# A tuned decoder kernel: the first conditioning's shift summed by TensorE, half of its tokens scaled by ScalarE

## The chip, the cores and the metric

One Trainium2 chip, one of its cores. The metric is the device time of one execution in microseconds, as a median over runs. All data is f32; some matmul operands are split into a high and a low fp32r part.

## The reference, cut to what matters

Two decoder layers over 256 tokens of width 1024. Each begins with an adaptive conditioning; of layer 0 only the first lines concern the change:

```
c_act = silu(c)                                   # (1, 1024)
mod   = c_act @ w_mod[l] + b_mod[l]               # (1, 6*1024): sh1, sc1, g1, sh2, sc2, g2
h     = x * (1.0 + sc1) + sh1                     # 256 tokens, 1024 wide
y     = hybrid_mixer(h, w_in[l], ...)             # h @ w_in, then attention and gated linear attention
x     = layer_norm(ALPHA * x + (1.0 + g1) * y, ...)
```

After the mixer come a SwiGLU of width 2816 (layer 0) and a mixture of experts (layer 1), about the last 770 us of the kernel.

## The kernel before, in words

All engines run programs of their own, and semaphores tie them together. The order of the work is written out by hand.

**First conditioning.** The 1024 rows of w_mod are cut into 8 blocks k of 128 rows (128 partitions), and of each block only the 1024 columns of the shift (a = 0) and of the scale (a = 1) are loaded first: 16 pieces of 512 KB, in the order of FIRST_ROWS (line 90), with the two halves of x behind pieces 10 and 12 (line 91, loop at line 375). SyncE issues them, and behind them the weights of the projections (`unit_load`, line 412). Before the change VectorE takes each piece as it lands (line 1463 on): it multiplies it by c_act's column k and adds it to `ycat[:, a, :]`, so that each partition holds a partial sum. TensorE then sums over partitions (`sum_chunk`, line 983): for each 128 columns, four products of 32 columns of the accumulator with a column of ones (`mm4`, line 938). Once both are summed, VectorE writes the conditioning into the table modT (line 1453). Between its two sums TensorE transposes x (`transposed_tokens`, 16 transposes into banks 0 to 3) and the table of norms (line 992).

**First tokens.** `modulate_first` (line 1497) makes hfull = x^T * scale + shift, a block kt of 128 columns of the model at a time, on VectorE alone. `project` for unit U_BQ (line 1017 on) multiplies hfull by the raw weights in f32: for ct = 0 and 1, the eight kt in order, each waiting for its block of hfull.

**What follows.** The units of the projection have a ring of four buffers. Unit u (from 4 on) is loaded once unit u - 4 is projected (line 414), so that unit 4 (U_IQ1) waits for unit 0 (U_BQ). ScalarE rounds a unit to its high part (`conv_unit`), VectorE subtracts (`low_unit`), and TensorE projects with three fp32r products (`mm3`). The tokens get a high and a low part too (`high_of_tokens`, `low_of_tokens`). SyncE's queue also carries the conditioning rows of later stages (`load_mod_rows`); rows 0 and 1 wait for the first sums (mod_ps), the others mostly for a buffer to be read (row_rd, VectorE's `condition_rows`). GpSimd (POOL) loads the gate's bias and the norm rows; it starts that once the first conditioning's partial sums are ready.

**Names and lines.** Piece loads L376 and L381, units L424, rows L409. Partial sums L1466 and L1469, sums over partitions L942, token transposes L951, table modT L1456, modulation L1501, U_BQ L1022, unit splits L651 (ScalarE) and L1552 (VectorE), token parts L692 and L1525, later rows L1539 and L1541, ScalarE's decay bias L711.

Of the kernel before, what the change touches and what calls it, by code (L numbers as in the profile page):

```python
# [21 lines left out]
ACT = mybir.ActivationFunctionType  # L22
AX = mybir.AxisListType

P = 128
D = 1024
KT = D // P
T = 256
# [61 lines left out]
FIRST_ROWS = [(1, k) for k in range(4)] + [(a, k + 4 * a) for k in range(4) for a in (1, 0)] + [(0, k) for k in range(4, 8)]  # L90
# [18 lines left out]
def hybrid_decoder(nc, x, c, w_in, w_a2, b_a, gla_norm_g, w_out, w_mod, b_mod, ln_g, ln_b,  # L109
# [3 lines left out]
    with ctx:  # L113
# [418 lines left out]
        def _(pool):  # L532
# [71 lines left out]
            pool.wait_ge(s["mod_sum"], 2)  # L604
# [23 lines left out]
        def _(act):  # L628
# [57 lines left out]
            def high_of_tokens(ph):  # L686
                for h in ((1, 0) if ph else (0, 1)):
                    if ph and h:
                        act.wait_ge(s["hfull_a"], ph * KT)
                    else:  # L690
                        act.wait_ge(s["hfull"], ph * KT + (KT if ph else 4 * h + 4))
                    A(hT_H[:, 4 * h:4 * h + 4, :], hfull[:, 4 * h:4 * h + 4, :], ACT.Copy).then_inc(s["hT_H"], 1)  # L692
# [110 lines left out]

            mixer(0)
# [130 lines left out]
        def _(pe):  # L935
# [29 lines left out]
            def token_tile(ph, t, kt):  # L965

                if kt < 4:
                    pe.wait_ge(s["hfull"], ph * KT + 4 * t + kt + 1)
                else:
                    pe.wait_ge(s["hfull_a"], (ph - 1) * KT + 4 * t + kt - 3)  # L970
# [17 lines left out]
            pe.wait_ge(s["mod_sum"], 1)  # L988
            sum_chunk(ycat[:, 1, :], bank[6][:, KT:2 * KT])
# [5 lines left out]
            pe.wait_ge(s["mod_sum"], 2)  # L995
            sum_chunk(ycat[:, 0, :], bank[6][:, 0:KT]).then_inc(s["mod_ps"], 1)

            def project(l, u, between=None):
                b = bank[4 + u % 2]
                if u < PLAIN:  # L1000
# [16 lines left out]
                    else:  # L1017
                        for ct in range(2):
                            for kt in range(KT):
                                if ct == 0:  # L1020
                                    pe.wait_ge(s["hfull"], kt + 1)
# [421 lines left out]
        def _(dve):  # L1443
# [17 lines left out]
            before = [0, 0]  # L1461
            for i, (a, k) in enumerate(FIRST_ROWS):
                dve.wait_ge(mod_ld[i], 16)
# [3 lines left out]
                else:  # L1467
                    dve.wait_ge(s["dve_chain"], before[a])
                    last = V.scalar_tensor_tensor(out=acc, in0=w, scalar=c_act[:, k:k + 1], in1=acc,  # L1469
                                                  op0=ALU.mult, op1=ALU.add)  # L1470
                if k == KT - 1:
                    last.then_inc(s["mod_sum"], 1)
                else:
                    last.then_inc(s["dve_chain"], 1)
                    n[0] += 1
                    before[a] = n[0]
                if i == 8:
# [19 lines left out]
            def modulate_first():  # L1497

                for kt in range(KT):
# [21 lines left out]
            def low_of_tokens(ph):  # L1521
                for i, h in enumerate((1, 0) if ph else (0, 1)):
# [503 lines left out]
```

## Time and profile before

| | |
|---|---|
| median of 3 runs | 1275.26 us (1275.22 to 1275.42) |
| the profiled execution's own time | 1272.66 us |
| its span | 1270.9 us |
| mean granted TensorE clock | 0.983 |
| TensorE matmul busy | 1183.0 us (93%) |
| VectorE busy | 569.0 us (45%) |
| ScalarE busy | 302.1 us (24%) |
| DMA, mean | 318 GB/s |

The profile is one execution. Its times are from the first to the last instruction (the span). PE is TensorE's matmuls, PEld its weight loads, DVE VectorE, ACT ScalarE, POOL GpSimd, SP SyncE; a "q" behind a name is that engine's queue issuing a transfer. A busy share is an average over stages. This change touches the first 50 us, so timelines and the chain of waits over that stretch say more than the page's totals. The granted clock is TensorE's, as a share of 2.4 GHz.

### The profile page before, as it was taken

To read this page: it belongs to the slowest core of one execution; us is meant where nothing else is said; L and a number is where in the kernel's file an instruction comes from. 1 tells how busy PE (TensorE), PEld (TensorE's weight loads), DVE (VectorE), ACT (ScalarE), POOL (GpSimd) and SP (SyncE) were. 2 spreads that over 40 slices of the span, in tenths; PEclk is the share of its full clock that TensorE was granted. 3 is DMA by queue.
4 is the path that set the end of the run, shared out by engine and by line. 5 is a ranking of instruction groups with operands and counts; after the bars stand their busy time and mean duration, and the time that the engine had idled before them with its cause. 6 is when DMAs were issued, how large, how long until landed. Compare 5 with 4: busy or idle time off the path is not lost.

```text
span 1270.9 us, 26228 instructions
## 1 busy us (share of the span) xinstructions
PE 1183.0 (93%) x11180; PEld 641.1 (50%) x11180; DVE 569.0 (45%) x913; ACT 302.1 (24%) x521; POOL 43.8 (3%) x84
## 2 busy tenths in 40 slices
PE   1889889999999898799999999999999999999996
PEld 1879867788878787523334323334233233333332
DVE  6799988677758999421021020111210210210224
ACT  0557243433336571310010010100100100100100
POOL 2101010000011010000000000000000000000001
PEclk9899989999999999799999999999999999999998
DMA  9973868899727648889999989999989999999950
GB/s 340 312 257 116 290 227 312 322 347 329 244 68 239 201 167 315 334 326 371 413 364 414 394 299 414 412 364 411 388 310 411 410 364 404 396 362 411 379 233 34
DMA packets 149083, 403.60 MB, mean 318 GB/s; under 512 B 19964, under 2 KB 71328, under 8 KB 137696
## 3 DMA queue, kind: packets, MB, share of 16 engines
q1 hardware_dynamic: 146720, 395.16, 82.5%
q0 software_dynamic: 2240, 6.68, 1.4%
q8 instruction: 92, 1.51, 0.5%
q14 instruction: 31, 0.25, 0.1%
HBM read 400.75 MB, written 1.05 MB: 316 GB/s over the span
## 4 chain that ended last, share of the span: by engine, by line
PE 75%; DVE 13%; DMA 6%; issue 3%; ACT 2%; SPq 1%; POOL 0%; DVEq 0%; ACTq 0%
PE bank L1349 36%; PE bank L1368 18%; PE bank L337 5%; PE bank L339 4%; PE bank L338 4%; DVE mod_acc L1541 3%; DMA raw_u<-in_ffn_w_up_dram 2%; DMA u_raw<-in_w_in_dram 2%; DVE u_low L1552 2%; PE bank L1331 1%; DMA mod_first<-in_w_mod_dram 1%; PE bank L1228 1%; DVE score L1596 1%; PE bank L1339 1%; PE bank L1022 1%
## 5 line engine op out<-in xcount | busy, mean ns | idle before, releaser
L1349 PE MATMUL bank<-raw_w,xg 128*32 128x512 f32 (+1 forms) x4608 | 462.9, 557 | 4.5 <-issue 2.5
L1349 PEld LDWEIGHTS bank<-raw_w,xg 128*32 128x32 f32 x4608 | 147.1, 110 | 304.7 <-issue 304.6
L1368 PE MATMUL bank<-raw_w,heT 128*32 128x512 f32 x2112 | 232.9, 593 | 0.0
L1915 DVE TENSOR_TENSOR he<-he,bank 128x256 f32<-128x256 f32 (+1 forms) x72 | 25.6, 384 | 369.4 <-ACT he L869 369.4
L869 ACT ACTIVATE he<-bank 128x256 f32<-128x256 f32 (+1 forms) x72 | 21.2, 367 | 542.8 <-PE bank L1349 542.8
L1368 PEld LDWEIGHTS bank<-raw_w,heT 128*32 128x32 f32 x2112 | 67.3, 110 | 150.5 <-issue 149.3
L1942 DVE SCALAR_TENSOR_TENSOR ycat<-bank,gate_tab,ycat 128x512 f32<-128x512 f32 x36 | 25.4, 747 | 173.0 <-PE bank L1340 171.1
L1541 DVE SCALAR_TENSOR_TENSOR mod_acc<-mod_row,c_act,mod_acc 128x1024 f32<-128x1024 f32 x70 | 89.8, 1283 | 6.8 <-DVE mod_acc L1541 0.9
L337 PE MATMUL bank<-u_high,hT_H 128*128 128x256 f32 x256 | 75.4, 294 | 4.9 <-DVE u_low L1552 3.5
L339 PE MATMUL bank<-u_high,hT_L 128*128 128x256 f32 x256 | 72.8, 284 | 0.0
L338 PE MATMUL bank<-u_low,hT_H 128*128 128x256 f32 x256 | 72.6, 284 | 0.0
L337 PE MATMUL bank<-gu_H,hT_H 128*128 128x512 f32 x160 | 64.8, 405 | 0.0
L651 ACT ACTIVATE u_high<-u_raw 128x2048 fp32r<-128x2048 f32 x26 | 49.7, 1912 | 59.6 <-DMA u_raw<-in_w_in_dram 45.6
L339 PE MATMUL bank<-gu_H,hT_L 128*128 128x512 f32 x160 | 63.1, 395 | 0.0
L338 PE MATMUL bank<-gu_L,hT_H 128*128 128x512 f32 x160 | 63.1, 394 | 0.0
L1552 DVE TENSOR_TENSOR u_low<-u_raw,u_high 128x2048 fp32r<-128x2048 f32 x26 | 59.2, 2286 | 3.0 <-ACT u_high L651 2.8
L337 PEld LDWEIGHTS bank<-u_high,hT_H 128*128 128x128 f32 x256 | 49.0, 191 | 8.0 <-DVE u_low L1552 4.6
L337 PE MATMUL bank<-hT_H,u_high 128*128 128x256 f32 x176 | 50.6, 287 | 2.1 <-DVE u_low L1550 2.1
L1926 DVE TENSOR_TENSOR y_sum<-y_sum,bank 32x512 f32<-32x512 f32 x48 | 32.9, 685 | 42.7 <-ACT y_sum L883 42.1
L339 PE MATMUL bank<-hT_H,u_low 128*128 128x256 f32 x176 | 49.6, 282 | 0.0
L338 PE MATMUL bank<-hT_L,u_high 128*128 128x256 f32 x176 | 49.5, 281 | 0.0
L338 PEld LDWEIGHTS bank<-u_low,hT_H 128*128 128x128 f32 x256 | 49.0, 192 | 0.7 <-issue 0.7
(284 smaller groups left out, 1378.7 us busy)
## 6 DMA issues: line engine op xcount, KB each, us to landing
raw_w<-in_moe_w_down_dram SPq DMA_DIRECT2D x88, 1024.0 KB, 8.6
raw_w<-in_moe_w_gate_dram SPq DMA_DIRECT2D x128, 512.0 KB, 8.5
raw_w<-in_moe_w_up_dram SPq DMA_DIRECT2D x128, 512.0 KB, 9.8
mod_row<-in_w_mod_dram SPq DMA_DIRECT2D x80, 512.0 KB, 6.4
raw_w<-in_moe_w_gate_dram SPq DMA_DIRECT2D x64, 384.0 KB, 5.6
raw_w<-in_moe_w_up_dram SPq DMA_DIRECT2D x64, 384.0 KB, 6.8
u_raw<-in_w_in_dram SPq DMA_DIRECT2D x20, 1024.0 KB, 7.5
raw_d<-in_ffn_w_down_dram SPq DMA_DIRECT2D x11, 1024.0 KB, 10.1
```

The costliest lines, as they stand in the source:

```text
L337: nc.tensor.matmul(out_ap, aH, bH, start=first, stop=False)
L338: nc.tensor.matmul(out_ap, aH, bL, start=False, stop=False)
L339: return nc.tensor.matmul(out_ap, aL, bH, start=False, stop=last)
L651: A(dst[:], src[:], ACT.Copy).then_inc(s["wH"], 1)
L869: A(he[:, g, 0:w].rearrange("s (j b c) -> s j b c", b=2, c=32), bank[g][:, 0:w].rearrange("s (j c b) -> s j b c", b=2, c=32), ACT.Silu).th ...
L1349: last = mm(bank[g][32 * q:32 * q + 32, 0:2 * HALF[c]].rearrange("s (m j r) -> s m j r", m=2, r=64), xg[:, i, k, 32 * g:32 * g + 32], cols ...
L1368: last = mm(bank[3 + g][32 * q:32 * q + 32, :], heT[(par + c) % 2][:, g, 2 * a + b, :], W[:, b, h * 512:(h + 1) * 512], start=(c == 0 and ...
L1541: last = V.scalar_tensor_tensor(out=acc, in0=row[:], scalar=c_act[:, k:k + 1], in1=acc, op0=ALU.mult, op1=ALU.add)
L1552: V.tensor_tensor(L[:], src[:], H[:].bitcast(F32), ALU.subtract).then_inc(s["wL"], 1)
L1915: V.tensor_tensor(h, h, bank[g][:, w:2 * w].rearrange("s (j c b) -> s j b c", b=2, c=32), ALU.mult).then_inc(s["m_hid"], 1)
L1926: last = V.tensor_tensor(a, a, bank[3 + g][64 * h + 32:64 * h + 64, :], ALU.add)
L1942: V.scalar_tensor_tensor(out=a, in0=bank[b][:], scalar=gate_tab[:, t, bass.ds(E, 1)], in1=a, op0=ALU.mult, op1=ALU.add).then_inc(s["m_acc" ...
```

## The change

FIRST_ROWS now goes through k, with the scale's piece ahead of the shift's. VectorE sums only the scale's pieces. TensorE forms the shift itself: for each landed piece k, eight products of 128 columns of raw weights with the column c_act[:, k], accumulated over k in bank 6 (`shift_row`). Six of the eight pieces stand ahead of the transposes, two behind them, and the scale's sum over partitions is last. modT follows it. Blocks 4 to 7 of the tokens are modulated by ScalarE, ahead of its first unit split, and signalled by hfull_a; U_BQ takes the blocks in the order 0, 4, 1, 5, 2, 6, 3, 7. The tokens' high and low parts go through the halves in the order 1, 0 in every phase. GpSimd waits for mod_ps in place of mod_sum.

```diff
--- before.py
+++ after.py
@@ -87,7 +87,7 @@
 ROWS_AT_STEP = (0, 5, 5, 5, 5, 4, 4, 4, 4, 4, 0)
 MOD_AT_STEP = {3: 5, 5: 6, 6: 7, 8: 8}
 
-FIRST_ROWS = [(1, k) for k in range(4)] + [(a, k + 4 * a) for k in range(4) for a in (1, 0)] + [(0, k) for k in range(4, 8)]
+FIRST_ROWS = [(a, k) for k in range(KT) for a in (1, 0)]
 X_AFTER = (9, 11)
 
 HF0, HF1, YC0, YC1, X0 = range(5)
@@ -601,7 +601,7 @@
                     link(pool.tensor_scalar(rms[:, t, :], ssq[:, t, :], 1.0 / B_DV, EPS, ALU.mult, ALU.add))
                     pool.tensor_tensor(rms[:, t, :], rms[:, t, :], half_neg[:, 4:8], ALU.pow).then_inc(s["rms"], 1)
 
-            pool.wait_ge(s["mod_sum"], 2)
+            pool.wait_ge(s["mod_ps"], 1)
             gate_bias(0, 2, g_row)
             mixer(0)
             norm_power(0)
@@ -684,11 +684,8 @@
                 last.then_inc(s["evac"], 1)
 
             def high_of_tokens(ph):
-                for h in ((1, 0) if ph else (0, 1)):
-                    if ph and h:
-                        act.wait_ge(s["hfull_a"], ph * KT)
-                    else:
-                        act.wait_ge(s["hfull"], ph * KT + (KT if ph else 4 * h + 4))
+                for h in (1, 0):
+                    act.wait_ge(s["hfull_a" if h else "hfull"], ph * KT + 4)
                     A(hT_H[:, 4 * h:4 * h + 4, :], hfull[:, 4 * h:4 * h + 4, :], ACT.Copy).then_inc(s["hT_H"], 1)
 
             def normalise(ph):
@@ -801,6 +798,11 @@
                         conv_unit(l, NIN + 2)
                 conv_unit(l, NIN + 3)
 
+            act.wait_ge(s["modT"], 1)
+            for kt in range(4, KT):
+                act.wait_ge(s["xT_ps"], kt // 2 + 1)
+                A(hfull[:, kt, :], bank[kt // 2][:, (kt % 2) * T:(kt % 2 + 1) * T], ACT.Identity,
+                  scale=modT[:, 8 + kt:9 + kt], bias=modT[:, kt:kt + 1]).then_inc(s["hfull_a"], 1)
             mixer(0)
 
 
@@ -965,9 +967,9 @@
             def token_tile(ph, t, kt):
 
                 if kt < 4:
-                    pe.wait_ge(s["hfull"], ph * KT + 4 * t + kt + 1)
+                    pe.wait_ge(s["hfull"], ph * KT - 4 + 4 * t + kt + 1)
                 else:
-                    pe.wait_ge(s["hfull_a"], (ph - 1) * KT + 4 * t + kt - 3)
+                    pe.wait_ge(s["hfull_a"], ph * KT - 4 + 4 * t + kt - 3)
 
             def gate_sum(m, banks):
 
@@ -985,15 +987,26 @@
                 for k in range(KT):
                     last = mm4(o[:, k:k + 1], acc[:, k * P:(k + 1) * P], ones[:, 0:1], start=True, stop=True)
                 return last
-            pe.wait_ge(s["mod_sum"], 1)
-            sum_chunk(ycat[:, 1, :], bank[6][:, KT:2 * KT])
+
+            def shift_row(k):
+
+                pe.wait_ge(mod_ld[FIRST_ROWS.index((0, k))], 16)
+                for j in range(KT):
+                    mm(bank[6][:, j:j + 1], mod_first[:, k, j * P:(j + 1) * P], c_act[:, k:k + 1],
+                       start=(k == 0 and j == 0), stop=(k == KT - 1 and j == KT - 1))
+
+            pe.wait_ge(s["cact"], 1)
+            for k in range(6):
+                shift_row(k)
             pe.wait_ge(s["cols_rd"], 1)
             pe.wait_ge(s["stage2_ld"], 32)
             nc.tensor.transpose(bank[7][:, 0:P], stage2[:], ident[:]).then_inc(s["stageT"], 1)
             pe.wait_ge(s["x_ld"], 32)
             transposed_tokens(x_sb, "xT_ps")
-            pe.wait_ge(s["mod_sum"], 2)
-            sum_chunk(ycat[:, 0, :], bank[6][:, 0:KT]).then_inc(s["mod_ps"], 1)
+            shift_row(6)
+            shift_row(7)
+            pe.wait_ge(s["mod_sum"], 1)
+            sum_chunk(ycat[:, 1, :], bank[6][:, KT:2 * KT]).then_inc(s["mod_ps"], 1)
 
             def project(l, u, between=None):
                 b = bank[4 + u % 2]
@@ -1016,9 +1029,9 @@
                             last = mm(b[q:q + BLK, 0:T], u_raw[u % 4][:, kt, 0:BLK], hfull[:, kt, :], start=(kt < 4), stop=(kt >= 4))
                     else:
                         for ct in range(2):
-                            for kt in range(KT):
+                            for kt in (0, 4, 1, 5, 2, 6, 3, 7):
                                 if ct == 0:
-                                    pe.wait_ge(s["hfull"], kt + 1)
+                                    pe.wait_ge(s["hfull" if kt < 4 else "hfull_a"], kt % 4 + 1)
                                 last = mm(b[:, ct * T:(ct + 1) * T], u_raw[u % 4][:, kt, ct * P:(ct + 1) * P], hfull[:, kt, :],
                                           start=(kt == 0), stop=(kt == KT - 1))
                     last.then_inc(s["proj"], 1)
@@ -1458,23 +1471,21 @@
 
 
             dve.wait_ge(s["cact"], 1)
-            before = [0, 0]
             for i, (a, k) in enumerate(FIRST_ROWS):
+                if a == 0:
+                    continue
                 dve.wait_ge(mod_ld[i], 16)
                 w, acc = mod_first[:, k, a * D:(a + 1) * D], ycat[:, a, :]
                 if k == 0:
                     last = V.tensor_scalar(acc, w, c_act[:, 0:1], None, ALU.mult)
                 else:
-                    dve.wait_ge(s["dve_chain"], before[a])
                     last = V.scalar_tensor_tensor(out=acc, in0=w, scalar=c_act[:, k:k + 1], in1=acc,
                                                   op0=ALU.mult, op1=ALU.add)
                 if k == KT - 1:
                     last.then_inc(s["mod_sum"], 1)
                 else:
-                    last.then_inc(s["dve_chain"], 1)
-                    n[0] += 1
-                    before[a] = n[0]
-                if i == 8:
+                    link(last)
+                if k == 4:
                     dve.wait_ge(s["stageT"], 1)
                     V.tensor_copy(cols[:], bank[7][:, 0:P]).then_inc(s["cols_rd"], 1)
             dve.wait_ge(s["cols_rd"], 1)
@@ -1496,7 +1507,7 @@
 
             def modulate_first():
 
-                for kt in range(KT):
+                for kt in range(4):
                     dve.wait_ge(s["xT_ps"], kt // 2 + 1)
                     V.tensor_scalar(hfull[:, kt, :], bank[kt // 2][:, (kt % 2) * T:(kt % 2 + 1) * T],
                                     modT[:, 8 + kt:9 + kt], modT[:, kt:kt + 1], ALU.mult, ALU.add).then_inc(s["hfull"], 1)
@@ -1519,7 +1530,7 @@
                 dve.wait_ge(s["lnm"], ph + 1)
 
             def low_of_tokens(ph):
-                for i, h in enumerate((1, 0) if ph else (0, 1)):
+                for i, h in enumerate((1, 0)):
                     k = slice(4 * h, 4 * h + 4)
                     dve.wait_ge(s["hT_H"], 2 * ph + i + 1)
                     V.tensor_tensor(hT_L[:, k, :], hfull[:, k, :], hT_H[:, k, :].bitcast(F32), ALU.subtract)\
```

## Rows read from the trace of the kernel before

**Rows 1.** The chain of waits, 20 to 62 us (start us, us, what).
```profile
9.30 16.00 DMA mod_first<-in_w_mod_dram
...
30.84 0.75 PE bank L942 x59
...
31.69 0.25 DVE modT L1456 x2
...
32.66 10.09 PE bank L1022 x32
...
42.76 6.01 DMA u_raw<-in_w_in_dram
...
48.80 1.93 ACT u_high L651
```

**Rows 2.** Timeline of VectorE, 21 to 56 us (start us, us, instructions, idle before).
```profile
21.54 2.56 DVE L1469 SCALAR_TENSOR_TENSOR ycat<-mod_first,c_act,ycat 128x1024 f32<-128x1024 f32 x2 [1.10 <-DMA mod_first<-in_w_mod_dram]
25.33 5.45 DVE L1469 SCALAR_TENSOR_TENSOR ycat<-mod_first,c_act,ycat 128x1024 f32<-128x1024 f32 x4 [1.24 <-DMA mod_first<-in_w_mod_dram]
...
31.97 3.71 DVE L1501 TENSOR_SCALAR hfull<-bank,modT 128x256 f32<-128x256 f32 x8
...
45.66 2.29 DVE L1552 TENSOR_TENSOR u_low<-u_raw,u_high 128x2048 fp32r<-128x2048 f32 x1 [2.09 <-ACT u_high L651]
...
50.74 2.29 DVE L1552 TENSOR_TENSOR u_low<-u_raw,u_high 128x2048 fp32r<-128x2048 f32 x1 [0.73 <-ACT u_high L651]
52.95 2.67 DVE L1541 SCALAR_TENSOR_TENSOR mod_acc<-mod_row,c_act,mod_acc 128x1024 f32<-128x1024 f32 x2
```

**Rows 3.** Timeline of TensorE's matmuls, 0 to 32 us.
```profile
8.54 0.47 PE L981 MATMUL bank<-ident,stage 128*128 128x128 f32 x1 [8.54 <-POOL half_neg L563]
...
22.87 1.03 PE L942 MATMUL bank<-ones,ycat 128*32 128x1 f32 x64 [13.86 <-DVE ycat L1469]
...
24.11 3.64 PE L951 MATMUL bank<-ident,x_sb 128*128 128x128 f32 x16
...
30.84 0.71 PE L942 MATMUL bank<-ones,ycat 128*32 128x1 f32 x64 [3.09 <-DVE ycat L1469]
```

**Rows 4.** Timeline of weight loads in narrow stretches: strips, then first and first two full-width.
```profile
22.87 0.95 PEld L942 LDWEIGHTS bank<-ones,ycat 128*32 128x32 f32 x64 [14.15 <-DVE ycat L1469]
...
32.63 0.29 PEld L1022 LDWEIGHTS bank<-hfull,u_raw 128*128 128x128 f32 x1 [1.16 <-DMA u_raw<-in_w_in_dram]
...
32.63 0.50 PEld L1022 LDWEIGHTS bank<-hfull,u_raw 128*128 128x128 f32 x2 [1.16 <-DMA u_raw<-in_w_in_dram]
...
46.37 0.19 PEld L1102 LDWEIGHTS bank<-baT,wa 128*128 128x128 f32 x1 [3.12 <-ACT baT L677]
...
46.37 0.30 PEld L1102 LDWEIGHTS bank<-baT,wa 128*128 128x128 f32 x2 [3.12 <-ACT baT L677]
```

**Rows 5.** Windows: stretch, us, PE PEld DVE ACT POOL busy (records), PEclk, DMA share, GB/s.
```profile
24.10:27.80 3.70, 3.65 (x17) 3.25 (x16) 2.36 (x2) 0.00 (x0) 0.00 (x0) 1.00 1.02 409
32.60:38.50 5.90, 5.84 (x14) 4.71 (x15) 3.08 (x7) 2.52 (x2) 4.55 (x9) 0.50 1.08 365
38.60:42.75 4.15, 4.15 (x23) 3.38 (x26) 3.88 (x3) 1.19 (x2) 0.00 (x0) 1.00 1.04 420
46.30:47.10 0.80, 0.73 (x3) 0.68 (x4) 0.80 (x1) 0.02 (x1) 0.00 (x0) 1.00 1.06 372
...
509.60:513.00 3.40, 2.96 (x73) 2.64 (x74) 1.11 (x5) 1.80 (x5) 0.00 (x0) 0.50 1.02 406
513.00:516.40 3.40, 3.40 (x75) 3.05 (x76) 1.54 (x10) 0.94 (x2) 0.00 (x0) 0.50 1.03 410
```

**Rows 6.** Timeline of ScalarE, 35 to 52 us.
```profile
37.80 1.99 ACT L692 ACTIVATE hT_H<-hfull 128x1024 fp32r<-128x1024 f32 x2
43.65 1.91 ACT L651 ACTIVATE u_high<-u_raw 128x2048 fp32r<-128x2048 f32 x1 [3.86 <-DMA u_raw<-in_w_in_dram]
...
50.62 0.82 ACT L711 ACTIVATE dec<-bank,cols 128x256 f32<-128x256 f32 x2
```

## The prediction

> **What bounds the kernel now.** I read the chain of waits first, from 9 to 56 us, then each engine's timeline over that stretch. The chain [rows 1] shows no free piece at the start. The first conditioning's weights arrive until VectorE can take its last four blocks at 25.33; then come TensorE's sums over partitions (30.84), the table modT (31.69) and the first projection U_BQ, 10.09 us long. The chain leaves U_BQ for a transfer: SyncE may issue the block of unit 4 (U_IQ1) only when U_BQ is through (42.76), the block lands 6.01 us later, ScalarE splits it, VectorE subtracts. What counts for the rest of the kernel is when VectorE gets at U_IQ1's low part, at 50.74 [rows 2]. Behind that point VectorE has no long gap, and the shift of this point is the shift of the end.
>
> VectorE's timeline [rows 2] also gives the arrivals. It restarts on landings at 21.54 (block 11) and 25.33 (block 13); blocks 12 and 13 and half of x, 512 KB each, lie between, so one piece takes 3.8/3 = 1.27 us, and block 16 lands near 25.3 + 3 x 1.27 = 29.1. VectorE's last operation began at 29.5. So **only some 1.7 us** of VectorE work (30.8 - 29.1) can be taken off behind the last landing.
>
> **What one single-column product costs.** Each f32 matmul is two weight loads and two matmul records (64 records for 32 products in each of the two sums [rows 3]). The old sums load 32 columns at a time, into four strips: 64 loads in 0.95 us. The new products load all 128 columns for one column of output, so the load is the price. No such product is in the trace; its load is. At a granted clock of 0.50 (1.2 GHz), the first full-width f32 load takes 0.29 us, two take 0.50; at 1.00 (2.4 GHz), 0.19 and 0.30 [rows 4, 5]. One more load costs 0.21 us or 0.11 us. The one-column matmul hides under the next load: the strips' 64 loads, four abreast, are 16 steps of 0.055 us for a quarter of the columns, in line with 0.21 for all. So a row block (8 products, 16 loads) costs 16 x 0.213 = 3.4 us at half clock or 1.76 us at full, and the shift's blocks come every 2.54 us (every second piece). Bounds for a load: 0.055 us below (if full width cost no more than a strip), 0.21 above.
>
> **The clock at that time.** The windows print 1.00 over 24.1 to 27.8 [rows 5], but 16 transposes take 3.64 us there, 0.21 us apart, and the sum of 22.87 takes 1.03 us where the same sum at 30.84 takes 0.71 [rows 3]. I read half clock up to the transposes and full clock after them. It is at 0.50 again over 32.6 to 38.5 and at 1.00 behind that [rows 5]. So the products begin cold. Do they raise the clock? In 509.6 to 513.0 TensorE was busy 2.96 of 3.40 us, most of the 73 records being the router's products of eight columns, and the clock was still 0.50 in the next stretch [rows 5], where the dense transposes had raised it near 28. [...] I take it that they don't raise it.
>
> **The change, step by step** (against the profiled execution).
> 1. TensorE is free for products from 8.54 + 0.47 = 9.0 [rows 3]; the first shift block lands by about 29.1 - 16 x 1.27 = 8.8. Six blocks at 3.4 us are 20.5 us: **29.5**, where the sixth landed at 22.8. TensorE is the bound now, not the transfers.
> 2. One stage transpose and the 16 token transposes, 17 x 0.213 = 3.6: 33.1, against 27.75 before.
> 3. The transposes raise the clock, as before. Blocks 7 and 8, long landed: 32 loads at 0.11 = 3.5 us: 36.6. They may start a little cold or end so.
> 4. The scale's sum, now last: 0.71 to 1.03, then 0.14 + 0.24 to modT [rows 1, 3]: **about 37.8**, against 31.93. That is +5.9 us.
> 5. VectorE loses 8 operations of at most 1.36 us each (5.45 / 4), some 10 us. Worth nothing: its last block is piece 15 now, landed at 27.8, done at 29.1, and it then waits for TensorE.
> 6. Modulation: 8 VectorE operations took 3.71 us [rows 2]; four now run on ScalarE, 0.41 us each by the nearest row, 128x256 out of PSUM with a bias [rows 6]. TensorE takes a block's first half in 0.85 us at half clock and 0.43 at full, VectorE gives one per 0.46: the split, with its new order of blocks, is worth at most 0.3 us.
> 7. U_BQ follows modT by 0.7 us as now: 38.5. Its 32 records move 256 columns each, twice a transpose's, so 0.427 us at half clock and 0.213 at full; 14 at the one and 18 at the other make 9.8, near the 10.09 measured, and 14 is what the window at 0.50 counts [rows 1, 5]. All at half is 13.7, all at full 6.8. It starts cold again after the narrow products; I take 9.3 (between 8.6 and 9.8). End **47.8** against 42.75, +5.0.
> 8. SyncE issues unit 4 at 47.8. The two mod_row blocks ahead of it, tied to the same modT sums, are through by then, where they were not before: 5.3 us in place of 6.01. Lands at 53.1, VectorE reaches U_IQ1 at 55.1 against 50.74: **+4.3 us**.
> 9. What stands in between is covered. ScalarE's split of U_BK sits behind its new modulation and runs at 39.5, not 36; then two token halves in 1.99 us, and the split of U_IQ0 at 43.5, when it ran at 43.65 anyway [rows 6]. VectorE's lows and two conditioning rows end near 51.4, before 55.1. TensorE's U_BK starts some 3.4 us late, less than VectorE. POOL now waits for the sums: its bias row, pads and row loads shift by 6 us and are needed much later. Swapping the halves of the tokens' high and low parts moves no end, since U_BK needs both.
>
> Sum: 1272.66 + 4.3 = 1277.0 for the profiled execution. The runs' median stands 2.6 us above it; on that scale 1275.26 + 4.3 = **1279.6 us**.
>
> **A rule beside the rows.** The rows give 0.21 us for a full-width f32 load at half clock and 0.11 at full. The Trainium skill, "TensorE: Matmul & The Clock Gate", LDWEIGHTS, has columns/1.2 ns, 107 ns for 128 columns, whatever the clock. By that rule TensorE would keep up; the row at half clock is twice that, and decides. The same page says of transposes (Part 4) that they don't count as busy for the clock; the sums before and after the transposes speak against it here, and by that rule step 3 would run cold, which is the second rival.
>
> **Rivals.**
> (a) *Clock stays low through blocks 7 and 8* (the transposes fall so that they don't raise it, or they count for less). 32 loads at 0.213 are 6.8, 3.3 more than above: modT at 41.1, and the end +7.6 us: 1282.9. For: the transposes stand between narrow work now. Against: the rise near 28.
> (b) *TensorE keeps up* (not slower). It decides at 2.54 us per block, 0.159 us a load: if a load of these takes 0.11 us at either clock, or the products raise the clock themselves, a block takes 1.76 us. Block 6 ends by 24.6, transposes by 28.2, blocks 7 and 8 at 31.6, modT at 32 to 33. U_BQ then ends between 40 and 43.1. A late end costs 0.3 us; an early one gives next to nothing, as VectorE, behind the U_IQ0 block that lands at 43.65, is not free before 50.74 - 0.73 = 50.0, and its next two rows wait on loads issued behind the last two. 1275.1 to 1275.6. For: loads cost 0.11 at full clock. Against: half clock at the start. (The skill's LDWEIGHTS rule above would give this case.)
> (c) *Faster.* The same, and U_IQ0's block also lands sooner because POOL's row loads no longer meet it. VectorE's gaps of 2.09 and 0.73 us [rows 2] are all there is: at best -2.8, 1272.5.
> (d) *Absorbed*: the delay arises, but a later wait on a transfer takes up part: +1 to +2.5.
>
> **Numbers.** The forecast 0.50 (1278.5 to 1281), (a) 0.24, (b) 0.17, (c) 0.03, (d) 0.06. A measurement of this kernel can tell about 0.2%, 2.5 us, from no change. Faster 0.03; same is (b) and (d) and a little of the forecast's low edge, 0.24; slower 0.73. The range 1275.1 to 1283.5 takes in (a) and most of (b).
>
> **What would show it.** Right: TensorE's product records back to back from 9 to about 29.5, weight loads of 128 columns 0.21 us apart; transposes ending near 33; modT near 38; U_BQ's end and unit 4's issue near 48. Wrong: gaps between the blocks of products (TensorE keeps up), loads nearer 0.11 or 0.055 us apart, or modT before 33. If modT is late and the end isn't, (d) holds.

## The result, and the profile after

The median of six runs is 1280.98 us, against 1275.24 us for six runs of the kernel before beside them: ratio 1.0053, 95% interval [1.0039, 1.0066]. The change costs 5.7 us by the medians, 6.8 by the ratio: half a per cent. The forecast was +4.3.

| | before | after |
|---|---|---|
| profiled execution's own time | 1272.66 us | 1287.19 us |
| its span | 1270.9 us | 1285.5 us |
| mean granted TensorE clock | 0.983 | 0.982 |
| TensorE matmul busy | 1183.0 us | 1212.3 us |
| VectorE busy | 569.0 us | 557.5 us |

The profiled execution of after is the slowest of its six, and that of before (1272.66) lies below all six runs beside after (1274.76 to 1276.59), so the 14.6 us between the spans is not the change's price. VectorE's instructions of the two traces, lined up with each other, say where it arises: after is 7.6 us late at 60 us, 9.5 at 540, 11.2 at 560, 12.6 behind the first of the experts' two loop jumps and 14.6 behind the second.

TensorE's matmuls in the timeline of after, to 52 us:

```profile
8.68 3.41 PE L995 MATMUL bank<-c_act,mod_first 128*128 128x1 f32 x16
12.81 17.23 PE L995 MATMUL bank<-c_act,mod_first 128*128 128x1 f32 x80 [0.72 <-DMA mod_first<-in_w_mod_dram]
...
30.14 3.62 PE L953 MATMUL bank<-ident,x_sb 128*128 128x128 f32 x16
33.56 6.83 PE L995 MATMUL bank<-c_act,mod_first 128*128 128x1 f32 x32
40.31 1.03 PE L944 MATMUL bank<-ones,ycat 128*32 128x1 f32 x64
42.45 8.68 PE L1035 MATMUL bank<-hfull,u_raw 128*128 128x256 f32 x32 [1.11 <-DVE hfull L1512]
```

Six blocks of products run from 8.68 to 29.9 with one gap of 0.72 us for a landing: 96 records, 0.215 us each. Blocks 7 and 8 run at the same 0.213 us a record; the transposes ahead of them didn't bring the full clock. The level is read off this spacing, which is that of the loads at a recorded 0.50 in [rows 4, 5]: the windows of a profile print 1.00 until its first recorded change of the clock, and that of after is a rise at 45.6 us. The sum (1.03) answers to the cold one of [rows 3] (cold: at half clock), and modT's first write comes at 41.49 (VectorE's timeline, next), 9.8 us later than in [rows 1].

VectorE's timeline of after over the same stretch:

```profile
29.58 1.28 DVE L1482 SCALAR_TENSOR_TENSOR ycat<-mod_first,c_act,ycat 128x1024 f32<-128x1024 f32 x1 [1.27 <-DMA mod_first<-in_w_mod_dram]
...
41.49 0.24 DVE L1469 SCALAR_TENSOR_TENSOR modT<-bank,cols 128x8 f32<-128x8 f32 x2 [10.62 <-PE bank L944]
41.76 1.90 DVE L1512 TENSOR_SCALAR hfull<-bank,modT 128x256 f32<-128x256 f32 x4
...
58.32 2.29 DVE L1563 TENSOR_TENSOR u_low<-u_raw,u_high 128x2048 fp32r<-128x2048 f32 x1 [2.77 <-ACT u_high L651]
```

The 10.62 us in front of modT are the VectorE time that the change freed: it became idle time. U_IQ1's low part begins at 58.32, not 50.74 [rows 2]: +7.6. ScalarE's timeline shows its new work and then the block it waits for:

```profile
41.76 1.93 ACT L804 ACTIVATE hfull<-bank,modT 128x256 f32<-128x256 f32 x4 [35.81 <-DVE modT L1469]
...
56.38 1.91 ACT L651 ACTIVATE u_high<-u_raw 128x2048 fp32r<-128x2048 f32 x1 [3.79 <-DMA u_raw<-in_w_in_dram]
```

SyncE issued that block at 51.17, when U_BQ was through; it landed 5.2 us later.

This is the course of rival (a), to 0.6 us: modT written by 41.7 (41.1 there), +7.6 at U_IQ1. A second execution of the same kernel, `r_after` below, took the course of the main forecast. Both are this kernel.

### The profile page after: what moved, and what is told of

It is laid out like the page before. It is cut to its first block, busy times and chain, and to the rows that moved or that the text cites. A ratio compares the mean times of both kernels' runs of the same rounds, so it can differ in the third digit from the quotient of the medians.

```text
span 1285.5 us, 26343 instructions
## 1 busy us (share of the span) xinstructions
PE 1212.3 (94%) x11244; PEld 669.1 (52%) x11244; DVE 557.5 (43%) x901; ACT 303.8 (24%) x525; POOL 43.8 (3%) x84
## 4 chain that ended last, share of the span: by engine, by line
PE 69%; DVE 6%; DMA 2%; issue 1%; ACT 1%; POOL 0%; SPq 0%; DVEq 0%; ACTq 0%
PE bank L1362 36%; PE bank L1381 18%; PE bank L337 3%; PE bank L339 3%; PE bank L338 3%; PE bank L1344 2%; DVE u_low L1563 1%; DMA u_raw<-in_w_in_dram 1%; PE bank L1352 1%; DMA raw_u<-in_ffn_w_up_dram 1%; DVE mod_acc L1552 1%; PE bank L1353 1%; DVE score L1607 0%; PE bank L944 0%; PE bank L977 0%
## 5 line engine op out<-in xcount | busy, mean ns | idle before, releaser
L651 ACT ACTIVATE u_high<-u_raw 128x2048 fp32r<-128x2048 f32 x26 | 49.7, 1913 | 28.2 <-PE bank L339 14.8
```

The costliest lines, as they stand in the source:

```text
L651: A(dst[:], src[:], ACT.Copy).then_inc(s["wH"], 1)
```

## The experiments

All ratios are to the kernel before on the same chip. Where a mark is named (U_IQ1's low part at 50.74 before, or modT's first write at 31.69), it is from one profiled execution.

**`r_after`: the change again**, for a second profile.

> The changed kernel unaltered, for a second profiled execution on the same chip. The first profile has VectorE 7.5 us late at U_IQ1's low part and another 7 us that arise after 540 us, while its timed runs are 5.7 us slower. If the late 7 us belong to one execution, this one's shift stays at 7 to 8 us or less to the end; if they follow from the change, it grows again in the experts. Timed 1280.5 to 1281.5.

Measured (four runs): 1282.94 us, ratio 1.0062 [1.0045, 1.0078]; the medians lie 8.4 us apart, and the time is above the range that I expected. Timelines of TensorE and VectorE, and a window behind blocks 7 and 8 (granted clock: third number from the end):

```profile
33.38 3.89 PE L995 MATMUL bank<-c_act,mod_first 128*128 128x1 f32 x32
39.27 9.56 PE L1035 MATMUL bank<-hfull,u_raw 128*128 128x256 f32 x32 [1.10 <-DVE hfull L1512]
...
38.31 0.24 DVE L1469 SCALAR_TENSOR_TENSOR modT<-bank,cols 128x8 f32<-128x8 f32 x2 [7.68 <-PE bank L944]
56.00 2.29 DVE L1563 TENSOR_TENSOR u_low<-u_raw,u_high 128x2048 fp32r<-128x2048 f32 x1 [3.63 <-ACT u_high L651]
...
37.20:43.90 6.70, 5.60 (x76) 4.65 (x76) 2.75 (x7) 5.32 (x7) 5.12 (x10) 0.51 0.95 335
```

The clock came up behind the transposes this time: the same 32 records in 3.89 us, 0.12 each, and it is recorded as back at half from 37.3 on. modT's first write is at 38.31, U_IQ1 +5.3. So the clock at blocks 7 and 8 came out differently in two executions of one kernel, and was worth 3 us at modT and 2.3 at U_IQ1. The other profiles say how often: behind the 16 transposes the clock came up in four of the twelve that entered them cold (before, `r_after`, `e_act_only`, `e_strips_old`) and stayed at half in eight; `e_wide` was up before. Before's second sum at 0.71 us [rows 3] is the rarer course: in `b_pad`, `b_hold2`, `e_hold` and `e_hold2` the same sum takes 1.03.

The growth behind 540 us, too, came back in this profile (1.7 us before 560, then 1.5 and 1.4 at the experts' jumps).

**`e_strips`: the same products in four strips of 32 columns**, so that a load costs what the old sums' loads did.

```diff
-                    mm(bank[6][:, j:j + 1], mod_first[:, k, j * P:(j + 1) * P], c_act[:, k:k + 1],
+                    mm4(bank[6][:, j:j + 1], mod_first[:, k, j * P:(j + 1) * P], c_act[:, k:k + 1],
...
```

> The changed kernel with one edit: each of the shift's products is cut into four strips of 32 output columns (64 weight loads of 32 columns per row block in place of 16 of 128). Theory A (the full-width f32 weight load at half clock, 0.213 us, sets the delay): a row block costs 1.0 us in place of 3.4, below the 2.54 us between its arrivals, so TensorE waits for each block; the last ends 1 us behind its landing near 29, modT at 31 to 32, and the time is that of the kernel before, 1275.2 within 1 us. Theory B (the delay comes from the new order, transposes and the scale's sum behind six blocks, or from POOL's and the mod_row loads tied to modT, or from ScalarE's modulation): it stays at 1279 to 1281.

Measured: 1279.22 us, ratio 1.0034 [1.0021, 1.0047]. TensorE's and VectorE's timelines:

```profile
20.26 1.03 PE L944 MATMUL bank<-c_act,mod_first 128*32 128x1 f32 x64 [0.89 <-DMA mod_first<-in_w_mod_dram]
...
31.61 1.03 PE L944 MATMUL bank<-c_act,mod_first 128*32 128x1 f32 x64 [0.59 <-DMA mod_first<-in_w_mod_dram]
...
33.64 0.24 DVE L1469 SCALAR_TENSOR_TENSOR modT<-bank,cols 128x8 f32<-128x8 f32 x2 [2.08 <-PE bank L944]
52.68 2.29 DVE L1563 TENSOR_TENSOR u_low<-u_raw,u_high 128x2048 fp32r<-128x2048 f32 x1 [3.05 <-ACT u_high L651]
```

A block takes 1.03 us instead of 3.4, TensorE waits for landings, and modT comes 8 us sooner than in after. The price of a full-width load is what makes modT late. But modT is still 1.9 us later than before with TensorE keeping up: the last block starts at 31.61, on a landing that I had placed at 29.1. And the time, 4.3 us above before by the ratio, misses theory A's 1275.2: only 1.9 us of that stands at U_IQ1 (52.68), the rest comes in the experts (below).

**`e_wide`: each load followed by 128 equal columns instead of one**, to see what the operand's width does to the clock.

```diff
-                    mm(bank[6][:, j:j + 1], mod_first[:, k, j * P:(j + 1) * P], c_act[:, k:k + 1],
-                       start=(k == 0 and j == 0), stop=(k == KT - 1 and j == KT - 1))
+                    mm(bank[4 + j // 4][:, (j % 4) * P:(j % 4 + 1) * P], mod_first[:, k, j * P:(j + 1) * P], c_wide[:, k, :],
+                       start=(k == 0 and j % 4 == 0), stop=(k == KT - 1 and j % 4 == 3))
...
```

(VectorE writes the 128 equal columns, `c_wide`, ahead of its sums, and reads the shift from banks 4 and 5 in place of bank 6.)

> The changed kernel, but each product moves 128 equal columns of c_act in place of one (f32, into banks 4 and 5; the shift is read from one column of each block). The weight loads are the same in number and width, and 128 moving columns take no longer than such a load. Theory A with the clock as its cause: the array now streams, the granted clock goes to full within the first blocks, a load costs 0.11 us, TensorE keeps up with the blocks from then on, modT at 31.5 to 33 us, U_BQ starts at full clock; 1274.5 to 1276. Rival (a full-width load of this kind costs 0.21 us at either clock, or the moving columns add to it): modT at 40 or later and 1280 to 1283.

Measured: 1277.36 us, ratio 1.0022 [1.0008, 1.0036]. TensorE's timeline, and two windows of its first three blocks:

```profile
9.90 8.03 PE L996 MATMUL bank<-c_wide,mod_first 128*128 128x128 f32 x48 [1.30 <-DVE c_wide L1477]
...
24.38 2.05 PE L996 MATMUL bank<-c_wide,mod_first 128*128 128x128 f32 x16 [1.71 <-DMA mod_first<-in_w_mod_dram]
26.37 1.91 PE L954 MATMUL bank<-ident,x_sb 128*128 128x128 f32 x16
32.34 2.05 PE L996 MATMUL bank<-c_wide,mod_first 128*128 128x128 f32 x16 [2.12 <-DMA mod_first<-in_w_mod_dram]
36.20 7.14 PE L1036 MATMUL bank<-hfull,u_raw 128*128 128x256 f32 x32 [1.17 <-DVE hfull L1520]
...
9.90:14.00 4.10, 4.10 (x19) 4.10 (x20) 1.89 (x2) 0.00 (x0) 0.00 (x0) 1.00 0.99 392
14.80:18.00 3.20, 3.12 (x27) 2.93 (x26) 1.91 (x2) 0.00 (x0) 0.00 (x0) 1.00 1.02 410
```

128 times the arithmetic, and faster than after. The first three blocks come at 0.167 us a record on average: 19 in the first 4.1 us (0.216), 27 in the 3.2 us behind 14.8 (0.12); the first recorded rise lies between the two windows, at 15.0. Later blocks come at 0.128, and U_BQ, which finds the clock up, takes 7.14 us where the cold starts took 8.6 to 10.1. One-column products kept TensorE busy from 8.7 to 29.9 with no rise recorded; the same loads with 128 columns behind them had one at 15.0. And at the start, cold, a record with 128 columns takes no longer (0.216) than one with a single column (0.213): the columns moved don't set the spacing there, and the strips show that the load does. modT's first write is at 35.18, later than in `e_strips`, since the last piece lands at 32.3; U_IQ1's low part is at 52.69, the same. The time is 1.4 us above the range expected; the experts' jumps (below) account for 2.7.

**`e_half`: half of the shift's products left out** (four of eight per block; the shift isn't computed, modT takes the scale's sum in its place).

```diff
-                for j in range(KT):
+                for j in range(0, KT, 2):
...
```

> The changed kernel with half of its shift products left out (columns 1, 3, 5, 7 of each block; modT takes the scale's sum for the shift too, so the shift is not computed). A block is then 8 weight loads, 1.71 us at half clock, below the 2.54 us between arrivals, and TensorE has as many instructions ahead of the experts' loop as the kernel before, modulo 256. Theory A (the load at half clock): TensorE keeps pace with the landings, modT at 31 to 33 us, U_IQ1's low part 0 to 2.5 us later than before, time 1275 to 1277. Theory F: gaps at the two jumps back of 2.2 to 2.45 us. Rival (order and dependences are what costs, not the loads): modT past 36, 1279 or more.

Measured: 1276.27 us, ratio 1.0008 [0.9998, 1.0018], the time that theory A gave. TensorE's timeline shows 8 records in 1.87 us and a wait for the landing before them, VectorE's shows modT at 33.73:

```profile
23.82 1.87 PE L995 MATMUL bank<-c_act,mod_first 128*128 128x1 f32 x8 [1.89 <-DMA mod_first<-in_w_mod_dram]
...
33.73 0.24 DVE L1469 SCALAR_TENSOR_TENSOR modT<-bank,cols 128x8 f32<-128x8 f32 x2 [3.48 <-PE bank L944]
52.42 2.29 DVE L1563 TENSOR_TENSOR u_low<-u_raw,u_high 128x2048 fp32r<-128x2048 f32 x1 [2.53 <-ACT u_high L651]
```

modT and U_IQ1's low part are those of `e_strips` within 0.3 us, yet `e_strips` is 3.3 us slower by the ratios, whose intervals don't meet. The two profiles differ by 2.7 us at the experts' jumps, below, which fits; the profiled `e_half` is the slowest of its eleven runs and has fallen 2.7 us behind `e_strips` by 500 us, so that the two spans are alike (1277.8 and 1277.5).

**`e_act_only`: only ScalarE's half of the modulation**, with the sums and the order of pieces of before.

```diff
-FIRST_ROWS = [(a, k) for k in range(KT) for a in (1, 0)]
+FIRST_ROWS = [(1, k) for k in range(4)] + [(a, k + 4 * a) for k in range(4) for a in (1, 0)] + [(0, k) for k in range(4, 8)]
...
-            for k in range(6):
-                shift_row(k)
+            sum_chunk(ycat[:, 1, :], bank[6][:, KT:2 * KT])
...
-            shift_row(6)
-            shift_row(7)
+            pe.wait_ge(s["mod_sum"], 2)
+            sum_chunk(ycat[:, 0, :], bank[6][:, 0:KT]).then_inc(s["mod_ps"], 1)
...
```

> Only the second half of the change: the partial sums as in the kernel before (both on VectorE, TensorE sums over partitions), but ScalarE modulates blocks 4 to 7, U_BQ takes the blocks in the order 0, 4, 1, 5, the halves go 1, 0, and POOL waits for mod_ps. Theory A: TensorE, at half clock, takes 0.85 us per block where VectorE gives one per 0.46, so nothing is gained or lost: 1275.2 within 0.6 us. Theory B (ScalarE's modulation or the swapped halves cost by themselves): 1276 to 1278. Rival C (the split is worth something): 1274 to 1274.9.

Measured: 1274.43 us, ratio 1.0000 [0.999, 1.001]; U_IQ1's low part at 50.50 (50.74 before). The split is worth nothing that can be measured, and all of the loss comes from the shift's products and the order around them.

**`e_pad` and `b_pad`: 128 idle TensorE instructions** (64 loads, 64 matmuls into a bank nobody reads) behind the last sum, in after and in before. After has 128 TensorE instructions more than before ahead of the experts' loop; the pad makes it 256, and gives before 128.

```diff
+            for _ in range(8):
+                mm4(bank[5][:, 0:1], ones[:, 0:P], ones[:, 0:1], start=True, stop=True)
```

> The changed kernel with 128 more TensorE instructions that do nothing of use (8 x 4 strip products of ones into bank 5), placed behind the last sum where TensorE waits for VectorE anyway. In the profiles so far the kernels with shift products (all with 128 instructions more than a multiple of 256 ahead of the experts' loop) show gaps of 2.8 to 3.4 us behind the loop's two jumps back, inside the gate and up products, and the kernels without them 2.2 to 2.45 us right at the jump; from there they are 1.3 to 2 us later per jump. Theory F (where the loop lies in the instruction stream sets the time to refetch it): with 128 more the gaps are 2.2 to 2.45 again and the time is 2.5 to 3.5 us below the changed kernel's: 1278 to 1280. Rival (the gaps come from the late start, or by chance): gaps near 3, time as the changed kernel, 1281 to 1283.

> The kernel before with the same 128 idle TensorE instructions behind its last sum. Theory F: the gaps behind the two jumps back grow to 2.8 to 3.4 us and the time by 2.5 to 3.5 us, to 1277 to 1278, with the first 60 us unchanged. Rival: no change, 1274.6 to 1275.2.

Measured: `e_pad` 1280.61 us, ratio 1.005 [1.0034, 1.0067]; `b_pad` 1277.56 us, 1.001 [1.0000, 1.0021]. The idle times at the jumps are as theory F has them in `e_pad` (2.14 and 2.25 us), a little short of it in `b_pad` (2.54 and 2.48); `e_pad`'s time misses it. The rows are TensorE's weight loads around the loop's jump back in the experts: the same two instructions in each kernel, with the gap between them. Before:

```profile
699.86 0.30 PEld L1331 LDWEIGHTS bank<-one_P,xH 128*128 128x128 f32 x2 [0.84 <-issue]
733.34 0.16 PEld L1349 LDWEIGHTS bank<-raw_w,xg 128*32 128x32 f32 x8 [2.21 <-issue]
746.85 0.19 PEld L1339 LDWEIGHTS bank<-yH,one_S 96*128 96x128 f32 x1 [0.84 <-issue]
```

After:

```profile
711.05 0.30 PEld L1344 LDWEIGHTS bank<-one_P,xH 128*128 128x128 f32 x2 [0.84 <-issue]
746.84 0.15 PEld L1362 LDWEIGHTS bank<-raw_w,xg 128*32 128x32 f32 x7 [2.81 <-issue]
759.43 0.19 PEld L1352 LDWEIGHTS bank<-yH,one_S 96*128 96x128 f32 x1 [0.84 <-issue]
```

`e_pad`:

```profile
707.00 0.30 PEld L1346 LDWEIGHTS bank<-one_P,xH 128*128 128x128 f32 x2 [0.84 <-issue]
740.40 0.16 PEld L1364 LDWEIGHTS bank<-raw_w,xg 128*32 128x32 f32 x8 [2.14 <-issue]
753.91 0.19 PEld L1354 LDWEIGHTS bank<-yH,one_S 96*128 96x128 f32 x1 [0.84 <-issue]
```

First row to last takes 46.99 us before, 48.38 after and 46.91 in `e_pad`. The same two instructions around both jumps, in all kernels:

| kernel | TensorE instructions against before | first jump, us | second jump, us |
|---|---|---|---|
| before | 0 | 46.99 | 46.87 |
| `b_hold2` (below) | 0 | 46.90 | 47.02 |
| `e_hold` (below) | 0 | 46.91 | 46.72 |
| `e_hold2` (below) | 0 | 46.77 | 47.02 |
| `e_act_only` | 0 | 47.11 | 47.06 |
| `e_half` | 0 | 47.10 | 47.04 |
| `e_pad` | +256 | 46.91 | 47.02 |
| `e_strips_old` (below) | +1024 | 46.90 | 46.91 |
| `b_pad` | +128 | 47.71 | 47.65 |
| `e_wide` | +128 | 48.24 | 48.28 |
| after | +128 | 48.38 | 48.86 |
| `r_after` | +128 | 48.49 | 48.29 |
| `e_strips` | +896 | 48.50 | 48.40 |

Multiples of 256 cost next to nothing (0.3 us at most), the others 1.5 us (`b_pad`) to 3.4 us (after) over the two jumps; `e_wide`, `r_after` and `e_strips` pay 2.7, 2.9 and 3.0. The thirteen traces show this without exception; why `b_pad` pays half of what after pays for the same count stays open. The traces' transfer records show what moves: instruction fetches of 16,384 bytes begin some 5.1, 17.0, 30.6 and 36.2 us behind the first row in all eight kernels with a multiple of 256, and some 9.1, 21.8, 33.2 and 38 us behind it in the five others. The Trainium skill, "Advanced Engine Details and Errata", ISA Cache, gives a line of the engines' instruction cache as 16 KB, 256 instructions; the size of the fetches and the period seen here agree, though no run varied the count finely enough to show where a line begins. The medians bear the effect out only in part: `e_strips` against `e_half` 3.3 us, `b_pad` 1.3 us by its ratio (2.5 by the medians), with an interval that begins at none. `e_pad` gained nothing that could be measured over after; its profile has the cold course (modT's first write at 41.01, U_IQ1's low part at 58.20), and then no growth in the experts: 7.5 us late at 60 us, 7.2 at the end.

**`e_strips_old`: strips, the old order of pieces, the scale's sum ahead of the transposes, and the pad**, meant to undo both losses at once.

```diff
-FIRST_ROWS = [(a, k) for k in range(KT) for a in (1, 0)]
+FIRST_ROWS = [(1, k) for k in range(4)] + [(a, k + 4 * a) for k in range(4) for a in (1, 0)] + [(0, k) for k in range(4, 8)]
...
-            for k in range(6):
+            for k in range(4):
                 shift_row(k)
+            pe.wait_ge(s["mod_sum"], 1)
+            sum_chunk(ycat[:, 1, :], bank[7][:, P:P + KT])
...
-            shift_row(6)
-            shift_row(7)
-            pe.wait_ge(s["mod_sum"], 1)
-            sum_chunk(ycat[:, 1, :], bank[6][:, KT:2 * KT]).then_inc(s["mod_ps"], 1)
+            for k in range(4, KT):
+                last = shift_row(k)
+            last.then_inc(s["mod_ps"], 1)
...
```

(`shift_row` has `mm4` as in `e_strips`; the pad follows.)

> Strip products for the shift, with the pieces in the order of the kernel before, four shift blocks and the scale's sum ahead of the transposes, the last four blocks behind them, and 128 idle instructions behind the last. Theory A with F: the last four shift blocks land 1.3 us apart; a block takes 1.0 us at half clock and 0.55 at full, so modT at 30.5 to 32.3 us against 31.9, and the rest as the kernel before: 1273.5 to 1275.5. If the pieces land late in this order too, the cause of the later landings (32.1 against 29.2) is not the order; if the time stays at 1278 to 1279, as with strips in the new order, Theory F is wrong or something else in the new products costs.

Measured: 1280.79 us, ratio 1.0039 [1.0024, 1.0053], a clear miss. TensorE's timeline:

```profile
35.26 1.71 PE L944 MATMUL bank<-c_act,mod_first 128*32 128x1 f32 x114 [3.86 <-issue]
40.37 0.91 PE L944 MATMUL bank<-ones 128*32 128x1 f32 x52 [3.22 <-issue]
41.21 9.94 PE L1039 MATMUL bank<-hfull,u_raw 128*128 128x256 f32 x32
```

TensorE stood still for 3.86 and 3.22 us with no semaphore to wait for, amid hundreds of short instructions. I read this as TensorE waiting for its own instructions to be fetched, while transfers keep the DMA engines full (the window's DMA share, last but one, is 1.09). The DMA view of each gap (31.4 to 35.2 and 37.2 to 40.3 us) has one instruction fetch in it, at 32.91 and 37.94 (queue, kind: packets, MB, share):

```profile
33.60:37.00 3.40, 1.74 (x128) 1.74 (x128) 0.00 (x0) 0.00 (x0) 0.00 (x0) 0.50 1.09 379
...
q8 instruction: 1, 0.02, 1.6%
...
q8 instruction: 1, 0.02, 1.9%
```

TensorE starts again 2.4 us behind the beginning of each. No run took the transfers away to prove it. The first gap sent modT's first write to 37.15. The second lies inside the pad (the rows of `ones`) and held U_BQ back until 41.21, so part of this miss is the pad's own doing.

**`e_hold`, `e_hold2`, `b_hold2`: GpSimd's row loads held back**, so that they don't meet the blocks of units 3 and 4. `e_hold` and `e_hold2` are `e_act_only` with a wait for ScalarE's unit splits; `b_hold2` is before with it.

```diff
+                else:
+                    pool.wait_ge(s["wH"], 3)
```

(3 in `e_hold`, 10 in the other two.)

> The kernel with the old sums and ScalarE's half of the modulation (1274.4), and POOL's two row loads and gnorm (1.1 MB) held until ScalarE has split U_IQ1 (wH 3). Theory G: U_IQ1's block, issued at U_BQ's end, lands late because those loads and mod_row 0 and 1 are served with it; without 1.1 MB it lands up to 2 us sooner (4 us behind its issue, not 5.6), and as VectorE waits 2.5 us for it, the end is 1.5 to 2 us sooner: 1272.5 to 1273. Rival (the block's time is its own, or VectorE's next rows are what is late): 1274.4 within 0.5.

> As e_hold, but POOL's row loads wait until ScalarE has split ten units (near 97 us, where the DMA engines have room). Theory G: U_IQ1's low part starts near 49.0 as in e_hold, and the 1.1 MB no longer meet the blocks of U_IQ1, U_KEYS and U_AQ0, so the 1.5 us stay: 1272.7 to 1273.7. Rival: another block or row is late and takes them back: 1274.4 to 1275.2.

> The kernel before with the same hold and nothing else. If the hold is worth it by itself: 1273 to 1274; if ScalarE's half of the modulation is needed with it, 1274.5 or more.

Measured: `e_hold` 1275.73 us, ratio 1.0008 [0.9998, 1.0018]; `e_hold2` 1272.09 us, **0.9986 [0.9976, 0.9997]**; `b_hold2` 1274.36 us, 0.9998 [0.9988, 1.0008]. In `e_hold` VectorE reached U_IQ1 at 49.04, 1.7 us sooner than before and 1.5 sooner than `e_act_only`, and then ScalarE waited for the next block:

```profile
49.04 2.29 DVE L1564 TENSOR_TENSOR u_low<-u_raw,u_high 128x2048 fp32r<-128x2048 f32 x1 [1.08 <-ACT u_high L653]
...
59.18 1.06 ACT L651 ACTIVATE u_high<-u_raw 128x1024 fp32r<-128x1024 f32 x1 [5.08 <-DMA u_raw<-in_w_in_dram]
```

The held loads (1.1 MB on GpSimd's queue between 48 and 60 us) met a later block, and the gain was gone by 68 us. Little of it was the hold's in the first place: U_BQ took 8.56 us there and 9.71 in `e_act_only`, and the block of U_IQ1 landed 5.2 us behind its issue, against 5.6. So theory G's 1.5 to 2 us from an earlier landing is wrong; the landing gives 0.4. `e_hold2` holds them past all units. It is the only kernel here whose interval lies ahead of before, by 0.14%, and beats after by more than 0.5%. But its own profile has U_IQ1's low part at 50.71, where I expected 49 (its U_BQ took 10.07 us, the landing 5.4), so why it is faster stays open, and among a dozen intervals one that just leaves out no change can be chance; alone, the hold does nothing that can be told (`b_hold2`).

## Why the prediction was right, and where not

The sign, the place and the mechanism held, and 1280.98 us lies 1.4 us from the 1279.6 forecast. That it lies so close is partly luck: the second measurement of the same kernel is 8.4 us above its before, the profiled after took a course 3.3 us longer than the forecast's, and a term of some 3 us was left out (both below). Step by step:

1. *A block costs 16 loads of 0.213 us.* Right: 96 records to 29.9 (29.5 forecast). `e_strips` and `e_half` show that it is this price that makes TensorE the bound. Rival (b) fell. (The strips' 0.95 us over 16 steps is 0.059 us a step, not 0.055; nothing hangs on it.)
2. *Transposes end at 33.1.* 33.7: they started later, and took the same 3.6 us.
3. *The transposes raise the clock.* In `r_after` yes (3.89 us, 3.5 forecast), in the profiled after and in `e_pad` no (6.8, as rival (a) had it). "As before" leaned on one execution, whose course only four of twelve took. I had these as two cases, one of them true; they are two courses of one kernel, and the right figure for a median lies between +4.3 and +7.6 from this cause. The row at 509.6 that was read for narrow products says little of them: by records most of it is the router's, but two thirds of its busy time are transposes, as TensorE's timeline of before shows. That one-column products leave the clock low was right all the same, by after's first 21 us.

```profile
510.04 1.94 PE L961 MATMUL bank<-ident,ycat 128*128 128x128 f32 x8 [2.16 <-ACT ycat L698]
511.91 1.04 PE L942 MATMUL bank<-wr,hfull 128*32 128x8 f32 x64
```

4. *modT near 37.8.* 38.5 or 41.7.
5. *VectorE's ten microseconds are worth nothing.* Right: 10.62 and 7.68 us of idle time ahead of modT. But its last piece landed and started at 29.5, where I had 27.8 (see below); it mattered to nothing, since TensorE was later.
6. *The modulation's split is worth at most 0.3 us.* `e_act_only`: ratio 1.0000, with 0.1% on either side. ScalarE took 0.45 us a block from start to start, 0.41 estimated.
7. *U_BQ takes 9.3 us, 8.6 to 9.8.* 8.68 and 9.56: cold at first, as said.
8. *U_IQ1's block lands 5.3 us after its issue, VectorE arrives at 55.1.* 5.2 us (the 5.3 had no row behind it), and 56.0 or 58.3. That a shift of this point is the shift of the end was only half right: from 60 to 500 us VectorE's instructions, lined up with before's, stay 7 to 9 us late in after and 5 to 7 in `r_after` (9.5 and 7.9 at 540); behind that the experts add their own part.

**Two terms were missing**, each of 2 to 3 us and so not to be seen in the total. First, *the last landing was placed at 29.1*, from the old order's spacing. Where TensorE keeps up, the last block starts on its landing at 31.6 (`e_strips`) and 32.3 (`e_wide`), and modT comes 1.9 and 3.5 us late even so. For the change itself this was covered, since TensorE reached block 8 later still; for rival (b) it means that "TensorE keeps up" was never worth nothing. The landing events of the traces say more. With the old order and no shift products the last piece lands at 29.2 to 29.6 (before, `b_hold2`, `e_act_only`), in `e_half` at 30.2, in after and `r_after` at 32.2 and 32.1. Pieces follow each other by 1.3 us; in after and `r_after` the last step is 2.7 and 2.8 us, and an instruction fetch of 16 KB begins in it, at 29.8 and 29.5. In `e_half`, with half of the products, the first such fetch comes at 33.7, behind all pieces, and no step is long. `e_strips`, `e_wide` and `e_strips_old` have one long step each near a fetch, the last of these with the old order. So a fetch is the likely cause of the long step, some 1.4 us in after. It isn't shown: a fetch at 29.3 in `e_pad` delayed nothing (last piece at 30.3), and no run moves the fetch alone. The rest of the lateness is there by the fourth piece (landed at 11.2 to 11.5 in those three, at 12.2 to 12.8 in every kernel of the new order), and why stays open. Second, *step 9 took everything behind U_IQ1 to be carried over unchanged*. With its 128 more TensorE instructions the two stretches around the experts' jumps back are 2.9 to 3.4 us longer, 700 us behind the last edited line. I had counted the instructions by their time alone.

A further 1.7 us, between 540 and 565 us, belongs to neither. TensorE's granted clock in the windows of after, and of `e_half`, over the same stretch (before prints 1.00 there, too):

```profile
561.00:564.40 3.40, 3.40 (x24) 0.86 (x20) 2.81 (x7) 2.00 (x4) 0.00 (x0) 0.50 0.87 339
```

```profile
561.00:564.40 3.40, 3.40 (x34) 0.99 (x30) 2.67 (x5) 1.05 (x2) 0.00 (x0) 1.00 0.82 250
```

3.4 us at half clock cost 1.7 us. `e_act_only`, which is no slower than before by its median, has the same step in its profile, and so have seven others, `b_hold2` and `b_pad` among them; before's hasn't. It is luck of an execution, before's this time, and part of why the two profiled spans lie further apart than the medians.

The sum is then: 5.3 or 7.6 us at U_IQ1 (the two courses, against the one profile of before), some 3 from the experts, against 5.7 by the medians (6.8 by the ratio, interval 5.0 to 8.4) and, in `r_after`, 8.4 (7.9, interval 5.7 to 9.9). These add up to 8 to 11 us, more than was measured in either, and `e_pad`, which takes the second away in its profile, didn't come out faster than after. How the two parts share the 5.7 us stays open.

**The two rules beside the rows.** The load rows: 80 full-width f32 loads of after in the stretch of half clock:

```profile
12.81 17.14 PEld L995 LDWEIGHTS bank<-c_act,mod_first 128*128 128x128 f32 x80 [0.81 <-DMA mod_first<-in_w_mod_dram]
```

17.14 / 80 = 0.214 us each; in `e_wide`, clock up, 16 records take 2.05. The rule of the Trainium skill, "TensorE: Matmul & The Clock Gate", LDWEIGHTS (columns/1.2 ns, with no word on the clock), gives 0.107 and would have made rival (b) right; the measurement decides against it at half clock. The same page says in Part 4 that transposes don't count as busy for the clock, by which step 3 runs cold: that is rival (a), the first in the list and not, as the prediction has it there, the second. That fits the profiled after and seven others; `r_after` contradicts it, where nothing but transposes and one-column products stand ahead of the full-clock blocks, and so do before, `e_act_only` and `e_strips_old`, where the first recorded rise comes within 0.6 us of the transposes' end.

## What to carry to other kernels

A matrix-vector product on TensorE is paid in weight loads: put the price of a full-width load at the clock that holds there beside the interval of the landings, and narrow strips (1.03 us a block here against 3.4) or the vector engine beside it. Freeing an engine that waits for a transfer anyway buys nothing (10 us of VectorE here), and handing that work to the engine in front of the next transfer's release costs at once. Before you write "as before" of the clock, read it in more than one profile. When instructions are added ahead of a long loop, look at the time around its jumps back in both traces before you explain the end by the edited lines.

## What was not expected of the hardware

- The time around a loop's jump back went with how many TensorE instructions stand ahead of the loop: 46.7 to 47.1 us with none or a multiple of 256 more, 47.7 to 48.9 with 128 or 896 more.
- TensorE stood idle with no semaphore shown: 3.86 and 3.22 us in the middle of short strips (`e_strips_old`), with an instruction fetch in each gap.
- One-column products in a row, 96 records over 21 us, left TensorE at the half clock's spacing (0.215 us); 48 records with 128 columns did not (0.167 us a record over the first 48, 0.128 later).
- The clock behind the same 16 transposes came out at half in one execution and full in the next: 6.83 and 3.89 us for the same 32 records. It was at half in eight of twelve.
